# Constant matmuls on TensorE in seven pauses around the layer norms of a two-block network

## The reference, cut to what matters

```python
def first_block(...):
    h = _layer_norm(x) * (1 + sc1) + sh1
    y = _token_mixer(h, ...)
    x = _layer_norm(DEEPNORM_ALPHA * x + g1 * y, post1_g[l], post1_b[l])
    h = _layer_norm(x) * (1 + sc2) + sh2
    y = _moe(h, w_router[l], ...)
    x = _layer_norm(DEEPNORM_ALPHA * x + g2 * y, post2_g[l], post2_b[l])
...
def second_block(x, p, ...):
...
        x = layer_norm(DEEPNORM_ALPHA_2 * x + h, ln_gain[i, 0], ln_bias[i, 0])
        ff = squared_relu_mlp(x, mlp_w1[i], mlp_w2[i])
        pe = jax.nn.sigmoid(x @ ple_gate_w[i] + ple_gate_b[i]) * (p[i] @ ple_proj[i])
        x = layer_norm(DEEPNORM_ALPHA_2 * x + ff + pe, ln_gain[i, 1], ln_bias[i, 1])
```

## Time and profile before

| | |
|---|---|
| median of 3 runs | 2313.61 us (2311.02 to 2316.53) |
| profiled execution, its own time | 2318.56 us |
| its span in the trace | 2316.8 us |
| TensorE busy | 2059.3 us (89%) |
| VectorE busy | 856.3 us (37%) |
| mean granted clock of TensorE | 0.94 |

### The profile page before, as it was taken

One profiled execution on the slowest core, in us unless ns is written; L12 is line 12 of the kernel. 1 busy time (PEld: TensorE's weight loads), 2 busy tenths in 40 slices (PEclk: granted clock), 3 DMA queues, 4 the chain that ended last, 5 costly groups with the idle time before them and its releaser, 6 DMA issues. The chain is left out here.

```text
span 2316.8 us, 27597 instructions
## 1 busy us (share of the span) xinstructions
PE 2059.3 (89%) x10805; PEld 1299.8 (56%) x10805; DVE 856.3 (37%) x1408; ACT 388.4 (17%) x467; POOL 61.7 (3%) x126
## 2 busy tenths in 40 slices
PE   5999995998989899989899898699988876769997
PEld 3758784333333333333333333489868765657986
DVE  1296335111111111111111112555557664544654
ACT  1011101000000000000000001145334421113541
POOL 2000002000000000000000000100000000000000
PEclk9999897999999999999999999799999886979999
DMA  9478333959999998999998957445554200124552
GB/s 361 163 277 285 122 113 128 386 238 411 421 420 420 420 421 351 393 420 420 420 420 334 387 222 290 141 131 186 194 163 146 91 1 1 55 69 135 183 200 73
DMA packets 142660, 579.94 MB, mean 250 GB/s; under 512 B 10521, under 2 KB 12041, under 8 KB 93259
## 3 DMA queue, kind: packets, MB, share of 16 engines
q1 hardware_dynamic: 135824, 563.12, 62.6%
q0 software_dynamic: 3552, 12.61, 1.7%
q10 hardware_dynamic: 3131, 1.98, 0.3%
HBM read 576.62 MB, written 1.05 MB: 249 GB/s over the span
## 5 line engine op out<-in xcount | busy, mean ns | idle before, releaser
L1000 PE MATMUL bank<-ring,area 128*64 128x512 f32 x1632 | 370.5, 609 | 0.7 <-issue 0.5
L224 DVE TENSOR_TENSOR ring_r<-ring,ring_r 128x2048 fp32r<-128x2048 f32 x92 | 210.8, 2292 | 209.4 <-ACT ring_r L221 208.6
L1000 PEld LDWEIGHTS bank<-ring,area 128*64 128x64 f32 x1632 | 124.4, 141 | 232.8 <-issue 229.4
L722 PE MATMUL bank<-area,ring 128*128 128x256 f32 x1024 | 232.1, 390 | 10.1 <-issue 8.2
L722 PEld LDWEIGHTS bank<-area,ring 128*128 128x128 f32 x1024 | 200.3, 196 | 43.2 <-issue 12.2
L1895 DVE TENSOR_SCALAR area<-bank 128x512 f32<-128x512 f32 x36 | 24.9, 691 | 524.2 <-PE bank L1000 524.2
L221 ACT ACTIVATE ring_r<-ring 128x2048 fp32r<-128x2048 f32 x92 | 175.8, 1912 | 234.4 <-PE bank L759 209.5
L756 PE MATMUL bank<-area_r,ring_r 128*128 128x256 f32 x704 | 200.7, 285 | 2.2 <-DVE area_r L1787 2.2
L758 PE MATMUL bank<-area_r,ring_r 128*128 128x256 f32 x704 | 199.4, 283 | 0.0
L759 PE MATMUL bank<-area_r,ring_r 128*128 128x256 f32 x704 | 199.3, 283 | 0.0
L1038 PE MATMUL bank<-ring,area 128*64 128x512 f32 x848 | 188.6, 595 | 0.5 <-DVE area L1909 0.5
(11 more groups left out here) (295 smaller groups left out, 2126.8 us busy)
## 6 DMA issues: line engine op xcount, KB each, us to landing
ring<-in_w_gu SPq DMA_DIRECT2D x182, 1024.0 KB, 14.2
ring<-in_w_dn SPq DMA_DIRECT2D x94, 1024.0 KB, 14.6
area<-in_w_gu SPq DMA_DIRECT2D x74, 1024.0 KB, 12.9
ring<-in_mlp_w SPq DMA_DIRECT2D x64, 1024.0 KB, 5.4
area<-in_w_dn SPq DMA_DIRECT2D x34, 1024.0 KB, 16.6
ring<-in_w_mod SPq DMA_DIRECT2D x24, 1024.0 KB, 7.9
ring<-in_w_in SPq DMA_DIRECT2D x24, 1024.0 KB, 9.0
ring<-in_gdn_w_in SPq DMA_DIRECT2D x16, 1024.0 KB, 5.5
```

The source lines that it names most:

```text
L224: nc.vector.tensor_tensor(unit_low(i), raw, unit_high(i), ALU.subtract).then_inc(w_split, 1)
L722: ins = mm(bank(g)[:, m * S:(m + 1) * S], u[k // UK][:, k % UK, c:c + P], xT[:, k, :], start=k == 0, stop=k == ND - 1)
L1000: ins = mm(bk[hf * BLK:(hf + 1) * BLK, :], x[:, kt, :], block_u[:, c:c + BANK], start=False, stop=kt == ND - 1)
```

## The change

A new function, `keep_clock`, claims a group of its own and issues a fixed number of f32 matmuls with the constant `ident` as the stationary operand and 512 columns of the constant masks `level` as the moving one. All go into the group's bank, each overwriting the one before; nobody reads it, and TensorE itself gives the bank back with the last. Seven calls stand ahead of stages that wait: 14 matmuls before `h2T`, 11 before `pooled`, 6 before each `xT_i`, 3 between `xT_i` and the wait for `late_in`, 7 before `x4T`. The seven new groups move later groups to other banks, so that the first gather of the experts picks its two banks from a list (`FIRST`, here 5 and 7 where it was 4 and 6).

```diff
+                        ... ("y_tok", 4), ("warm_h2", 1), ("h2T", 4),
...
         group("moe", 4, align=0)
+        group("warm_pool", 1)
         group("pooled", 4)
         group("pool_tok", 4)
         for i in range(2):
             if i == 1:
+                group("warm_x4", 1)
                 group("x4T", 4)
...
+            group(f"warm_xT_{i}", 1)
             group(f"xT_{i}", 4)
+            group(f"warm_x_{i}", 1)
             group(f"pT_{i}", 1)
...
+            def keep_clock(gname, times):
+
+                g = G(gname)
+                claim(pe, g)
+                row = level[:, 0:4, :].rearrange("p i t -> p (i t)")
+                for i in range(times):
+                    ins = mm(bank(g)[:, :], ident[:, :], row, start=True, stop=True)
+                    settle(ins)
+                    if i == times - 2:
+                        fills(ins, g)
+                empties(ins, g)
+
...
+            keep_clock("warm_h2", 14)
             to_features("h2T", tok(3), xn_ready, 2 * NT)
...
-                gather_pair((bX, bU)[dh], 0, dh)
+                gather_pair(banks[FIRST[dh]], 0, dh)
...
+            keep_clock("warm_pool", 11)
             pe.wait_ge(windows_ready, 1)
...
             def ffn(i):
+                keep_clock(f"warm_xT_{i}", 6)
                 to_features(f"xT_{i}", x_tok, x_ready, NT * (1 + 2 * i))
+                keep_clock(f"warm_x_{i}", 3)
                 pe.wait_ge(late_in, 224 + 48 * i)
...
+            keep_clock("warm_x4", 7)
             to_features("x4T", x_tok, x_ready, NT * 2)
```

More of the change, by code:

```diff
@@ L247, in build @@
                         ("mod2", 2), ("u", 4), ("g_a", 4), ("g_b", 4), ("mod2T", 2), ("convT", 4), ("mix", 4),
-                        ("w_b", 4), ("yaT", 4), ("w_a", 4), ("w_out", 4), ("y_tok", 4), ("h2T", 4),
+                        ("w_b", 4), ("yaT", 4), ("w_a", 4), ("w_out", 4), ("y_tok", 4), ("warm_h2", 1), ("h2T", 4),
                         ("router", 1), ("h2_tok", 4), ("g2_bc", 2), ("pos", 1), ("gateT", 1)):
@@ L487, in experts @@
                 last_block((e, 0))
+        FIRST = [b for b in range(BANKS // 2, BANKS)
+                 if b not in [G(x, i) % BANKS for x, i in (("g2_bc", 0), ("g2_bc", 1), ("gateT", 0))]][:2]
         block = ctx.enter_context(nc.Block())
@@ L1059, in _ @@
             pe.wait_ge(moe_dve, 1)
-            assert all(G("g2_bc", q) % BANKS not in (4, 6) for q in range(2)) and G("gateT") % BANKS not in (4, 6)
             for dh in range(2):
-                gather_pair((bX, bU)[dh], 0, dh)
+                gather_pair(banks[FIRST[dh]], 0, dh)
             emptied(pe, G("gateT"))
@@ L1931, in _ @@
                 link(v.tensor_copy(xg[:, 0, UK * dh:UK * (dh + 1), :],
-                                   banks[(4, 6)[dh]][:, :].rearrange("p (d s) -> p d s", s=2 * BLK)))
+                                   banks[FIRST[dh]][:, :].rearrange("p (d s) -> p d s", s=2 * BLK)))
             link(v.tensor_copy(expert_sel[:, :], expert_hot[:, 0:1].to_broadcast([96, BLK])))
```

## The result

The change made the kernel slower: 2327.91 us median (2323.45 to 2339.0, 20 runs) against 2318.32 us (2309.36 to 2331.16, 20 runs) before, a ratio of 1.0042 with a 95% interval of 1.0029 to 1.0056, about 9.6 us. The profiled execution of after took 2326.49 us.

What follows compares the result with a forecast made beforehand. TensorE was taken as the bound, busy 2059.3 of 2316.8 us, with gains only from a kept clock behind its pauses. Terms -2.7-0.3-0.2+1.5 = -1.7 us took the median 2313.61 to 2311.9 us, range 2304.5 to 2319.

Steps and rivals of the forecast that it cites:

- The second rival: Kept clock ends pooled early, the wait for L1981 grows to 3.6 us, pool_tok runs cold: 2318.4 us, chance 0.15.
- the term *pooled: At pooled and pool_tok: nothing won, pool_tok may start cold after a longer wait: +1.5 us, bounds 0 and +8.
- the sum: Terms for gate products, h2T, x4T and pooled added together: -1.7 us.
- The price: All of pool_tok at half clock: about 8 us, 6.8 from its 256-column instructions, the rest from one-row ones.
- The edge of the clock: Idle time on TensorE after which the clock falls: 1.6 us safe, 3.9 lost, 2.8 to 3.0 the edge.
- So 1.6 us is safe: The 1.6 us of idle left in front of xT_0 and xT_1 would keep the clock.
- Gate products: Behind pT_i in both feed-forward parts: a third of at most 8.2 us of cold time saved, -2.7 us.
- h2T: At h2T and the router: full clock in the transposes starts ScalarE's copies earlier: -0.3 us, bounds 0 and -5.
- x4T: At x4T: the copies could start 0.6 us sooner, -0.2 us.

Runs made afterwards that it cites:

- e5: Changed kernel with only the calls ahead of and behind xT_i in the feed-forward parts: 2319.04 us, ratio 0.9999 against before.
- e14: Changed kernel with only the five calls behind pool_tok (feed-forward parts and ahead of x4T): 2324.22 us, ratio 1.0005 against before.
- e2: Changed kernel with only the 11 constant matmuls ahead of pooled, other six calls removed: 2329.55 us, ratio 1.0056 against before.
- e4: Changed kernel with the one-row pooling bias product left out of pool_tok: 2322.05 us in one execution.
- e7: Kernel before, no constant matmuls, with the bias product of pool_tok over 128 rows instead of one: 2315.03 us, ratio 0.9983.
- e10: e9 without warm_pool, with 5 instead of 3 matmuls behind xT_i and 9 instead of 7 ahead of x4T: 2306.37 us, ratio 0.9958.
- e1: Changed kernel without the 11 constant matmuls ahead of pooled, other six calls kept: 2325.26 us, ratio 1.0016 against before.
- e6: e3 with larger counts: 13 matmuls ahead of pooled, 5 behind xT_i, 9 ahead of x4T: 2324.62 us, ratio 1.0025 against before.
- e13: Changed kernel with only the 14 constant matmuls ahead of h2T: 2327.8 us, ratio 1.0025 against before.
- e15: e1 once more, for a second trace: 2332.16 us.
- e3: Changed kernel plus an eighth call, 3 constant matmuls between pooled and the wait for the scaled products: 2318.53 us, ratio 1.0001 against before.
- e9: Changed kernel with the bias products of pool_tok and both gate products over 128 rows: 2314.01 us, ratio 0.9989 against before.
- e8: Kernel before, no constant matmuls, with bias products over 128 rows in pool_tok and both gate products: 2309.84 us, ratio 0.9956.

## Why the prediction was wrong

**The mechanism was named, its chance and price were not right.** The second rival has it in nearly every step: a kept clock ends `pooled` early (forecast near 1463.4 with a wait of 3.6 us; measured 5.60 us after its start and 3.24 us), the wait is still for L1981, `pool_tok` runs cold to its end. It got a chance of 0.15 and 2318.4 us. The measured median is 16.0 us above the forecast of 2311.9; 4.7 of that are the baseline, since three runs of before lay that far below the median of twenty, and 11.3 are the error on the change itself, +9.6 against -1.7.

**The step that failed** is the term *pooled* of the sum, "The same can befall the kernel before, in executions where the clock rises early in `pooled`, so only part of it is a difference: +1.5". The three traces of before and e5 have `pool_tok` at 1.00, only e14's is cold, while both traces with `warm_pool`, one-row matmuls and no bridge (after and e2) are cold. So most of it is a difference: +11.6 us between the traces, where the term had +1.5 and at most +8.

**The price was too small.** "All of it at half clock would cost about 8 us" came to 11.6: a group of six instructions takes 3.1 us (25.15 us for eight) against 1.7 (13.55 for eight). The forecast gave the one-row matmuls little more than 1 us of it; they took some 4.8, 0.3 us each.

**The edge of the clock.** It was looked for in the length of the idle time alone. After 1.14 us and more the clock fell when one-row matmuls followed; when full ones did, e4 fell and was back in 3 us, and e7 to e10 did not fall. In after and e4 the fall came within 0.5 us of the end of the idle time, but in e1, e2, e6, e13, e14 and e15 it came 2.0 to 2.7 us into `pool_tok`. So the idle time and the light work behind it count together, and the length of the idle time does not settle it: 0.87 us fell in e6, 0.88 us held in e5. "So 1.6 us is safe" did not hold either: in feed-forward 1 of after the clock fell during the transposes after 1.6 us of idle (0.80 over the stretch from 2090.84) and was back before the gate product.

**What held.** In the trace of after the constant matmuls cost nothing by themselves: none outlasted its pause, VectorE's times are unchanged, and e3 with three more is 9.4 us faster. That they never cost anything is not shown, as e9 is above e8 and e10. 22 instructions took 9.71 us, 0.88 us a matmul against 0.86 forecast. The transposes of `xT_0` end 1.0 us sooner and the transfer lands no sooner (8.7 us after the start of `xT_0`, against 7.9 to 8.1). *Gate products*, forecast -2.7: feed-forward 1 takes 2.7 to 3.5 us less, feed-forward 0 between +0.3 and -1.1; together -2.4 to -4.5. *h2T*, forecast -0.3: 22.5 us is within before's 21.7 to 22.5, nothing. *x4T*, forecast -0.2: the transposes' gain is not seen, and `qkv` starts cold, 0.67 in its first 5 us, 87.1 us to `z` against 85.4 to 87.0. The sum with the measured `pool_tok` in it, +11.6-3.4, is +8, near the 7.9 us between the two profiled executions and the 9.6 us of the medians. That the two traces agree so well is partly luck: the stages ahead of `y_tok` are 3.3 us shorter in after's and the experts 3.4 us longer.

The Trainium skill, "TensorE: Matmul & The Clock Gate", section "Part 4: PE-mode transpose", holds that transposes do not count as activity. The traces here are mixed. In before the clock rose while only transposes ran. After 1.6 us of idle the clock stayed up through the sixteen transposes in ten cases, among them `xT_0` of e4, e9 and e10, each eight in 1.09 us; it fell in them in five, `xT_1` of after, e1, e3 and e15 and `xT_0` of e3. So transposes are not without effect, but they do not hold the clock surely.

## What to carry to other kernels

Before keeping a clock alive ahead of a stage, ask what that stage waits for when it is faster: here it was held by VectorE anyway, so the gain became idle time in front of the next stage, and that stage was the one that could not bear it. Look for stages in which a good part of TensorE's time goes to matmuls of one row (bias products led by a row of ones): they can stay at 1.2 GHz for their whole length. Giving such a matmul all 128 rows, with zeros below the first row of the stationary matrix, made no matmul longer here, and the kernel with that edit alone was 10 us of 2318 faster (e8). No gain of the constant matmuls on top of it shows in the time (e10).

## What had not been expected of the hardware

A matmul of one row is dearer than one of 128 rows also at 2.4 GHz: 48 instructions of `pool_tok` took 13.55 us with 16 one-row ones and 10.62 us with 128-row ones of the same width, 0.18 us for each of the sixteen. And in after the clock stayed at 0.50 through 25.15 us of uninterrupted work of that mix, with TensorE busy in all of it, while it came back after 3.0 us in the same stage without the one-row matmuls.
